# The transposed inverse in the delta heads, made by transposing instead of by products of its own

## What is computed

```python
lower = jnp.where(strict, jnp.einsum('bhncd,bhnmd->bhncm', k_beta, k) * decay, 0.0)
a_mat = lower + jnp.eye(C, dtype=f32)
rhs = jnp.concatenate([v_beta, k_beta * jnp.exp(g)[..., None]], axis=-1)
sol = lax.linalg.triangular_solve(a_mat, rhs, left_side=True, lower=True, unit_diagonal=True)
```

## Time and profile before

| | us |
|---|---|
| median of the runs | 1242.63 |
| lowest and highest of them | 1241.88, 1243.87 |
| profiled execution, its own time | 1245.12 |
| its span | 1243.3 |
| TensorE busy in the span | 1102.6 (89%) |
| VectorE busy | 695.8 (56%) |
| GpSimd busy | 610.4 (49%) |
| ScalarE busy | 525.5 (42%) |

### The profile page before, as it was taken

How to read it: one execution, slowest core, us unless ns; L and a number is a source line. 1 busy time by engine, 2 the same in 40 slices (tenths; PEclk the granted TensorE clock), 3 DMA queues, 4 the chain that set the end, 5 groups by cost and what they waited for, 6 DMA issues and landing times.

```text
span 1243.3 us, 17351 instructions
## 1 busy us (share of the span) xinstructions
PE 1102.6 (89%) x5405; PEld 762.5 (61%) x5405; DVE 695.8 (56%) x1697; ACT 525.5 (42%) x1037; POOL 610.4 (49%) x448
## 2 busy tenths in 40 slices
PE   8989999999999999999987978879788797887776
PEld 5879999999999899995533424325243252342222
DVE  4635545555552322324766667666676667676654
ACT  4565566555565777521423333233323333232211
POOL 3376675577655666661343434434434343344431
PEclk9999999999999999999999999999999999999999
DMA  7353333233323343666999999999999999999996
GB/s 247 117 167 106 118 105 114 101 106 113 118 102 104 135 141 130 254 241 269 376 414 421 422 421 422 421 422 422 420 422 422 422 422 422 421 422 420 422 422 264
DMA packets 61014, 355.23 MB, mean 286 GB/s; under 512 B 7983, under 2 KB 8494, under 8 KB 27054
## 3 DMA queue, kind: packets, MB, share of 16 engines
q0 software_dynamic: 36864, 268.45, 52.1%
q1 hardware_dynamic: 24110, 86.27, 19.9%
HBM read 353.65 MB, written 1.05 MB: 285 GB/s over the span
## 4 chain that ended last, share of the span: by engine, by line
PE 60%; DMA 27%; issue 6%; ACT 3%; DVE 2%; POOL 1%; DVEq 0%; POOLq 0%; ACTq 0%; SPq 0%
DMA top<-peer_uv_dram,route 20%; PE ps L1874 13%; PE ps L1528 9%; PE ps L1529 9%; PE ps L1530 9%; DMA front<-peer_uv_dram,route 7%; PE ps L1840 4%; PE ps L1825 2%; PE ps L1688 2%; PE ps L1707 2%; PE ps L1706 2%; ACT top L879 1%; POOL split L933 1%; PE ps L1786 1%; PE ps L1663 1%
## 5 line engine op out<-in xcount | busy, mean ns | idle before, releaser
L933 POOL TENSOR_TENSOR split<-front,split 128x1024 fp32r<-128x1024 f32 x123 | 297.8, 2432 | 176.8 <-ACT split L565 176.7
L1874 PE MATMUL ps<-top 128*128 128x512 f32 x640 | 298.1, 604 | 93.3 <-ACT top L879 93.3
L983 POOL DMA_INDIRECT top<-peer_uv_dram,route x160 | 170.7, 1067 | 248.9 <-PE ps L1874 241.0
L1874 PEld LDWEIGHTS ps<-top 128*128 128x128 f32 x640 | 115.4, 189 | 263.4 <-ACT top L879 155.1
L1343 DVE CUSTOM_DVE_ANT_0 top<-top,scratch 128x1024 f32<-128x1024 f32 x160 | 196.0, 1225 | 126.0 <-DMA top<-peer_uv_dram,route 126.0
L1528 PE MATMUL ps<-split 128*128 128x256 f32 (+1 forms) x768 | 241.4, 314 | 6.6 <-POOL split L933 3.4
L1529 PE MATMUL ps<-split 128*128 128x256 f32 (+1 forms) x768 | 224.6, 292 | 0.0
L1530 PE MATMUL ps<-split 128*128 128x256 f32 (+1 forms) x768 | 224.5, 292 | 0.0
L879 ACT ACTIVATE top<-cst,route 128x128 f32<-128x128 f32 x256 | 88.7, 393 | 281.9 <-DVE route L1351 267.3
L565 ACT ACTIVATE split<-front 128x1024 fp32r<-128x1024 f32 x128 | 133.3, 1056 | 136.2 <-PE ps L1530 125.0
L1528 PEld LDWEIGHTS ps<-split 128*128 128x128 f32 x768 | 147.0, 191 | 13.6 <-issue 8.5
(11 more groups left out here) (281 smaller groups left out, 1599.6 us busy)
## 6 DMA issues: line engine op xcount, KB each, us to landing
front<-in_tiles_dram SPq DMA_DIRECT2D x80, 512.0 KB, 3.3
front<-branch_tiles_dram SPq DMA_DIRECT2D x24, 512.0 KB, 3.9
front<-in_w_in_dram SPq DMA_DIRECT2D x8, 512.0 KB, 4.1
front<-in_w_mem_kv_dram SPq DMA_DIRECT2D x8, 512.0 KB, 3.4
front<-kv_tiles_dram SPq DMA_DIRECT2D x8, 512.0 KB, 4.2
top<-in_w_out_dram SPq DMA_DIRECT2D x8, 512.0 KB, 5.3
rest<-peer_w_q_by_head_dram SPq DMA_DIRECT2D x3, 1024.0 KB, 8.9
gate_part<-peer_w_q_by_head_dram SPq DMA_DIRECT2D x3, 1024.0 KB, 16.3
```

The costliest lines, as they stand in the source:

```text
L933: pool.tensor_tensor(halves[i % 3][:, 1], raw[i % 3], halves[i % 3][:, 0], ALU.subtract).then_inc(lo_ready, 1)
L983: pool.indirect_dma_start(rows_uv[k % RING], None, peer_uv, bass.IndirectOffsetOnAxis(ap=idx[c][:, k:k + 1], axis=0)).then_inc(s_row[k % R ...
L1874: ins = pe.matmul(ps[:, 2 * c + half, :], diag[:, k % 8, :], rows_uv[k % RING][:, D + half * 512:D + (half + 1) * 512], start=False, stop= ...
```

## The change

Levels 1 to 5 no longer correct XT by a product and a subtraction. Instead, at the beginning of each level from 2 to 6, TensorE transposes X of both chunks into bank 3 (new signal `lvlT`) and VectorE copies the result to XT, ahead of the copy of Y. In level 1, XT is still the one that was built at level 0. Level 6, which corrects XT alone, keeps its product and subtraction. `lvlX` is signalled by the one subtraction that is left.

```diff
                 for s in range(1, LEVELS):
+                    if s > 1:
+                        on(dve, "lvlT", h * (LEVELS - 2) + (s - 2))
+                        dve.tensor_copy(XT, ps[:, 3, T:HT])
                     on(dve, "lvlY", h * (LEVELS - 1) + (s - 1))
                     dve.tensor_copy(Y, ps[:, 4, 0:T]).then_inc(done("lvlYc"), 1)
...
                     on(dve, "lvlZ", h * LEVELS + s)
                     if s < LEVELS - 1:
-                        dve.tensor_tensor(X, X, ps[:, 3, 0:T], ALU.subtract)
-                    dve.tensor_tensor(XT, XT, ps[:, 3, T:HT], ALU.subtract).then_inc(done("lvlX"), 1)
+                        ins = dve.tensor_tensor(X, X, ps[:, 3, 0:T], ALU.subtract)
+                    else:
+                        ins = dve.tensor_tensor(XT, XT, ps[:, 3, T:HT], ALU.subtract)
+                    ins.then_inc(done("lvlX"), 1)
...
                     on(pe, "lvlX", h * LEVELS + (s - 1))
+                    if s > 1:
+                        for c in range(NC):
+                            ins = pe.transpose(ps[:, 3, T + c * P:T + (c + 1) * P], X[:, c * P:(c + 1) * P], ident)
+                        ins.then_inc(done("lvlT"), 1)
                     for c in range(NC):
                         a, b = c * P, (c + 1) * P
                         ins = pe.matmul(ps[:, 4, a:b], BT[:, s, a:b], X[:, a:b], start=True, stop=True)
...
                     for c in range(NC):
                         a, b = c * P, (c + 1) * P
                         if s < LEVELS - 1:
-                            pe.matmul(ps[:, 3, a:b], XT[:, a:b], Y[:, a:b], start=True, stop=True)
-                        ins = pe.matmul(ps[:, 3, T + a:T + b], Y[:, a:b], XT[:, a:b], start=True, stop=True)
+                            ins = pe.matmul(ps[:, 3, a:b], XT[:, a:b], Y[:, a:b], start=True, stop=True)
+                        else:
+                            ins = pe.matmul(ps[:, 3, T + a:T + b], Y[:, a:b], XT[:, a:b], start=True, stop=True)
                     ins.then_inc(done("lvlZ"), 1)
```

More of the change, by code:

```diff
@@ L420, in hybrid_layer @@
                   "pnorm", "vtok_kept", "p_turned", "pT_ready",
-                  "conv0", "conv0v", "mv_kept", "taps", "conv3", "silu", "dn_sq", "dn_ss", "dn_std", "dn_rstd", "dn_kq",
+                  "conv0", "conv0v", "lvlT", "mv_kept", "taps", "conv3", "silu", "dn_sq", "dn_ss", "dn_std", "dn_rstd", "dn_kq",
                   "Gm_ready", "gdiff", "decay", "decay_masked", "dv_turned", "kq_dots0", "kq_dots1",
```

## The result

The changed kernel took 1231.12 us in the median of four runs (1228.99 to 1233.23), the kernel before 1242.26 beside it (four runs, 1241.70 to 1243.87). The ratio is 0.9909, 95% interval 0.9887 to 0.9931: 11.1 us faster, clear of the 0.2% that can be told from no change. The forecast was 1229.0, with a range of 1226 to 1236; the two medians lie 2.1 and 2.5 us above it.

The account below looks back on a forecast made before the run. TensorE's queue was taken to bound the eight delta heads. Removed products (17.8 us) plus the `lvlX` wait (4.6) less added transposes (8.8) gave 13.6 us off, so 1229.0 us, range 1226 to 1236.

Parts of the forecast that it names:

- What bounds the kernel: In the eight delta heads TensorE's queue sets the time: a microsecond off it is a microsecond off the time.
- The removed products: Levels 1 to 5 lose two float32 products each, ten a head: 17.8 us less on TensorE's queue.
- The transposes: Levels 2 to 6 get two transposes each at 0.11 us apiece on TensorE: 8.8 us more.
- The wait for `lvlX`: TensorE's wait of 0.115 us at levels 2 to 6 goes, as VectorE signals 0.34 us earlier: 4.6 us less.
- The moved copy: VectorE's copy of the transposes fits ahead of the copy of Y with 0.10 us left: no cost.
- rival A: VectorE's queue becomes the wait, each Y copy 0.34 us late: 9.0 us lost, 1238.0 us; chance 0.08.
- The tiles: GpSimd's weight tile 3 is still ready before TensorE needs it: the margin of 1.9 us becomes 0.7.
- From the profiled execution to the median: Profiled execution 1245.12 us less 13.6 is 1231.5; the median taken 2.5 us below it, 1229.0.
- B: Each transpose in the heads costs what a product does, leaving a gain of 4.6 us, 1238.0 us; chance 0.04.
- C: Transposes stand one after another at their 0.272 us duration: gain 0.6 us, 1242.0 us, no change; chance 0.04.
- D: Transposes bring TensorE's clock down, 3.4 us lost per fall, once a head 27 us: 1256 us; chance 0.04.
- The head's period: The period from one head's start to the next falls by 1.7 us from 38.66.

Follow-up runs that it names:

- late_taps: The changed kernel with VectorE's hand-over of the finished convolution (wait for its last tap, then signal to ScalarE) put behind the subtraction of level 5; 1231.37 us.
- again: The changed kernel measured once more, with no edit; 1231.51 us against 1243.41 for the kernel before.
- fine_fills: late_taps with the fill handed out by single products, one per level moved from X's side to Y's; 1227.06 us against 1243.26 before the change.
- fine_again: fine_fills measured once more, with no edit; 1227.19 us against 1240.87 for the kernel before.

## The prediction against the result

**What bounds the kernel.** Right. TensorE's queue set the time of the heads before and after, and each edit of TensorE's work moved the heads by its own length: by the periods 8.7 us more for 40 more pairs of transposes and 8.5 less without them (6.9 more and 8.4 to 8.8 less in the medians).

**The removed products** (17.8 us forecast). Eight passes in 0.90 us became four in 0.44. Right. No experiment takes the products out by themselves, but the rest of the account leaves 17.6 us for them: 12.0 in the heads, and 8.6 for the transposes and 1.1 for the hand-over less 4.1 for the waits.

**The transposes** (8.8). 1.06 to 1.09 us a head, 8.5 to 8.7. Right, and for the reason given: the step between loads and not the duration.

**The wait for `lvlX`** (4.6). By itself 0.51 us a head, 4.1: a little less than put down, 0.5 us in all. Right at levels 2 to 5. In front of level 6 the step failed: "That is even: no wait, and no slack either, in seven of the heads" rests on a subtraction that starts at about 193.15, right behind the taps. The row of before, 193.40, had 0.24 us between the taps' end and the subtraction, and I took all of it for a wait for TensorE, as the bracket in the earlier trace rows says. It was two waits of equal length: TensorE's products ended just then, and so did VectorE's wait for its own last tap. The products of this level were loaded at 192.20, 1.20 us before the subtraction, which is the distance at level 1 too (178.17 to 179.37), where VectorE had nothing else to do for 1.18 us:

```profile
178.17 0.30 PEld L1706 LDWEIGHTS ps<-rest 128*128 128x128 f32 x2
...
192.20 0.30 PEld L1706 LDWEIGHTS ps<-rest 128*128 128x128 f32 x2
```

The taps' hand-over ends at 193.16 + 0.23 = 193.39. Taking away the one wait left the other. The wait of 0.22 us before level 6 came back in seven heads; net of the 0.04 that its transposes give back it is 0.15 to 0.17 a head, 1.1 us, which `late_taps` got back. The heads gained 12.0 us and not 13.6: 1.1 of the difference is this hand-over, and 0.5 the smaller waits.

**The moved copy.** Right: it costs nothing, with 0.11 us of room where 0.10 was worked out; rival A didn't come up, and its mechanism costs 5 us where one copy more brings it about.

**The tiles.** GpSimd's low half of tile 3 was done at about 177.9 (three in a row from 175.52, 7.09 us) and TensorE loaded its first product at 178.53: a margin of 0.65, forecast 0.7.

```profile
175.52 7.09 POOL L933 TENSOR_TENSOR split<-front,split 128x1024 fp32r<-128x1024 f32 x3
...
178.53 0.19 PEld L1533 LDWEIGHTS ps<-split 128*128 128x128 f32 x1
```

**From the profiled execution to the median.** The forecast goes down to the profiled execution and back by 2.5 us, which cancels: it is the median before less 13.6. That was right to do, since the distance of a profiled execution from its median is no constant. The execution profiled before had the longest fall of the clock in its opening (0.83) and took 2.5 us more than the median then known; the one profiled after had a short one before 20 us and took 1.6 less than its own. Had only the two profiles been compared, the change would have looked worth 15.6 us.

**Rivals B, C and D.** B and C are excluded by the price of 0.11 us, D by the clock of 1.00 in the heads.

**The head's period.** The prediction's 38.66 us counted one pass too many (364.1 is the start of the second); 38.59 is right. The expectation for `again` took 38.66 over, and with it 12.4 us for the change in place of 12.0.

## What to carry to other kernels

When the engine that sets the time looks 100% busy, compare the steps between its weight loads with the pace of a full queue: the difference is the waiting, and where a signal can be given one instruction earlier, part of a large change's gain is there for the asking (4.1 of 12.0 us here). Before you bank on a wait that goes, ask what else ends at the same moment, an engine's wait for its own previous result among it; the row names only one of them. And price a transpose and a product by the step to the next load, not by the duration that is drawn.

## What the runs showed of the hardware

- A float32 transpose of 128x128 takes 0.11 us of TensorE's queue and a float32 product of the same size 0.22 (two passes), though each pass is drawn with 0.27.
- On VectorE a copy from `ps` of 128x256 takes 0.42 us but the next starts 0.33 to 0.34 after it; behind a wait for the end of VectorE's own last instruction and a signal, the next starts 0.23 after that end (185.23 to 185.46) and not 0.09 ahead of it.
- The clock can fall to 1.2 GHz for 3.6 or 6.8 us in the opening of one execution and not in that of another (0.91 in `fine_fills` and 1.00 in `fine_again`, the same kernel, from 20 to 40 us). With such a fall the heads start 1.2 to 4 us later.
